# A two-block network on one core: the state heads of block one woven with the attention in a fixed period, and its turned x, B and chunk states placed later in the order

## What is computed

```python
for i in range(DEPTH):                       # DEPTH = 2
    h = rms_norm(x, norm_mix_w[i])
    proj = jnp.einsum("bld,de->ble", h, w_in[i])
    q, k, v, z, xbc_raw, dt_raw = jnp.split(proj, split_at, axis=-1)
    ...
    attn_out = blocked_gqa(q, k, v)          # 8 query heads, 2 key heads, head size 64
    ssd_out = ssd_mixer(z, xbc_raw, dt_raw, conv_w[i], conv_b[i], ...)
    x = x + jnp.einsum("ble,ed->bld", jnp.concatenate([attn_out, ssd_out], -1), w_out[i])
    h = rms_norm(x, norm_ffn_w[i])
    x = x + (silu(h @ w_gate[i]) * (h @ w_up[i])) @ w_down[i]
```

## Time and profile before

| | |
|---|---|
| median of 3 runs | 3262.46 us (3255.55 to 3265.68) |
| profiled execution | 3256.09 us, of which the traced span is 3254.3 us |
| TensorE busy | 3041.3 us (93% of the span) |
| VectorE, ScalarE, GpSimd busy | 1896.9, 1123.2, 87.5 us |
| mean granted TensorE clock | 0.968 |

### The profile page before, as it was taken

How to read it: one execution, slowest core, us unless ns; L and a number is a source line. 1 busy time by engine, 2 the same in 40 slices (tenths; PEclk the granted TensorE clock), 3 DMA queues, 4 the chain that set the end, 5 groups by cost and what they waited for, 6 DMA issues and landing times. The chain is left out here.

```text
span 3254.3 us, 39867 instructions
## 1 busy us (share of the span) xinstructions
PE 3041.3 (93%) x16294; PEld 2688.1 (83%) x16294; DVE 1896.9 (58%) x2835; ACT 1123.2 (35%) x1660; POOL 87.5 (3%) x72
## 2 busy tenths in 40 slices
PE   7988999999879999999967779999999999999998
PEld 6767888887768888899955369999999978799997
DVE  5755775856555878765546664552554365455464
ACT  4443422234444222343335123221222345433232
POOL 0031000000140000000000000000000000000000
PEclk9998999999989999999979889999999999999999
DMA  3100554521102655422100111121112210223232
GB/s 129 46 33 15 177 177 141 197 84 59 40 14 88 197 181 188 149 65 98 65 13 1 57 71 52 65 69 57 64 67 64 95 51 1 68 81 103 85 99 84
DMA packets 73137, 275.80 MB, mean 85 GB/s; under 512 B 7835, under 2 KB 11419, under 8 KB 71804
## 3 DMA queue, kind: packets, MB, share of 16 engines
q1 hardware_dynamic: 72956, 273.25, 25.3%
HBM read 264.83 MB, written 8.39 MB: 84 GB/s over the span
## 5 line engine op out<-in xcount | busy, mean ns | idle before, releaser
L122 PE MATMUL banks<-normed_hi,weights_hi 128*128 128x384 f32 (+2 forms) x2672 | 888.2, 338 | 11.5 <-DVE normed_lo L866 11.5
L123 PE MATMUL banks<-normed_lo,weights_hi 128*128 128x384 f32 (+2 forms) x2672 | 885.4, 337 | 0.0
L104 ACT ACTIVATE weights_hi<-weights_raw 128x1024 fp32r<-128x1024 f32 (+3 forms) x365 | 395.6, 1084 | 1244.9 <-PE banks L125 1218.4
L125 PE MATMUL banks<-normed_hi,weights_lo 128*128 128x384 f32 (+2 forms) x2672 | 743.5, 338 | 0.0
L110 DVE TENSOR_TENSOR weights_lo<-weights_raw,weights_hi 128x1024 fp32r<-128x1024 f32 (+3 forms) x365 | 459.7, 1259 | 139.4 <-ACT weights_hi L104 136.0
L122 PEld LDWEIGHTS banks<-normed_hi,weights_hi 128*128 128x128 f32 x2672 | 504.5, 189 | 39.7 <-DVE normed_lo L866 12.2
L123 PEld LDWEIGHTS banks<-normed_lo,weights_hi 128*128 128x128 f32 x2672 | 506.4, 190 | 27.3
L125 PEld LDWEIGHTS banks<-normed_hi,weights_lo 128*128 128x128 f32 x2672 | 473.8, 190 | 27.6
L123 PE MATMUL banks<-hidden_lo,weights_hi 128*128 128x512 f32 (+1 forms) x880 | 323.0, 367 | 0.0
L122 PE MATMUL banks<-hidden_hi,weights_hi 128*128 128x512 f32 (+1 forms) x880 | 323.0, 367 | 0.0
L125 PE MATMUL banks<-hidden_hi,weights_lo 128*128 128x512 f32 (+1 forms) x880 | 294.7, 367 | 0.0
(11 more groups left out here) (439 smaller groups left out, 4224.0 us busy)
## 6 DMA issues: line engine op xcount, KB each, us to landing
weights_raw<-in_w_up SPq DMA_DIRECT2D x176, 512.0 KB, 3.4
ada_tiles<-in_ada SPq DMA_DIRECT2D x96, 512.0 KB, 3.5
weights_raw<-in_w_down SPq DMA_DIRECT2D x64, 704.0 KB, 4.0
weights_raw<-in_w_in SPq DMA_DIRECT2D x67, 512.0 KB, 3.4
weights_raw<-in_w_out SPq DMA_DIRECT2D x32, 512.0 KB, 3.4
x_kept<-x SPq DMA_DIRECT2D x2, 3072.0 KB, 10.5
x<-x_kept SPq DMA_DIRECT2D x1, 3072.0 KB, 9.7
weights_raw<-in_mla_down SPq DMA_DIRECT2D x6, 512.0 KB, 3.4
```

The source lines that it names most:

```text
L104: act.activation(self.hi[:, n % 2, 0:w], self.raw[:, n % 2, 0:w], ACT.Copy).then_inc(self.high_ready, 1)
L122: pe.matmul(out, self.hi[:, s, m], xh, start=k == 0, stop=False)
L123: pe.matmul(out, self.hi[:, s, m], xl, start=False, stop=False)
L125: mm = pe.matmul(out, self.lo[:, s, m], xh, start=False, stop=k == kt - 1)
```

## The change

It adds, removes and alters no instruction; it alters the numbers by which `weave` orders them, in `FirstMix`, and so in both layers. First, attention steps 21 to 28 are no longer due every 1.2 units but one per head, at `head(h) + 0.5` (`slot`), with their exponential, maximum and rows moved into the next head's period (`follows`). Second, within a period of a head the order is laid down anew on TensorE (`decays` of the next head ahead of the attention step), ScalarE (`diagonal` ahead of the exponential, then `decay` of the next head) and VectorE (`diag` first, `skip` of the head before ahead of `weigh`). Third, the turned x are due every 1.2 instead of every 0.6 units, and the turned B, the B, C scores and the chunk states 0.7 later.

```diff
-        self.pace, self.lag = 1.2, 1.0
+        self.pace, self.lag, self.free = 1.2, 1.0, 21
...
+    def slot(self, n):
+
+        if n < self.free:
+            return self.pace * n + self.lag + 0.5
+        if n < self.free + 8:
+            return self.head(n - self.free) + 0.5
+        return self.head(8) + 0.5 + self.pace * (n - self.free - 8)
+
+    def follows(self, n, early, late):
+
+        return self.head(n - self.free + 1) + late if self.free <= n < self.free + 8 else self.slot(n) + early
...
-            yield self.pace * n + self.lag + 0.5
+            yield self.slot(n)
...
-            yield self.pace * n + self.lag + 0.8
+            if self.free <= n < self.free + 8:
+                yield self.slot(n) + 0.4
+                copy(n)
+            yield self.follows(n, 0.3, 0.4)
             if n + 2 < STEPS:
                 exp(n + 2)
-            yield self.pace * n + self.lag + 0.9
-            copy(n)
+            if not self.free <= n < self.free + 8:
+                yield self.slot(n) + 0.4
+                copy(n)
             if n % 2 and n >= 5:
-                yield self.pace * n + self.lag + 1.1
+                yield self.follows(n, 0.6, 0.42)
...
-            yield self.pace * n + self.lag + 0.7
+            yield self.follows(n, 0.2, 0.3)
             if n + 2 < STEPS:
                 top(n + 2)
             if n:
-                yield self.pace * n + self.lag + 0.85
+                yield self.follows(n, 0.35, 0.35)
                 rows(n - 1)
             if n % 2 and n >= 5:
-                yield self.pace * n + self.lag + 1.2
+                yield self.follows(n, 0.7, 0.55)
...
-            yield 12 + 0.6 * t
+            yield 12 + 1.2 * t
...
-            yield 19.3 + 0.5 * g
+            yield 20.0 + 0.5 * g
...
-            yield 20.3 + 0.5 * g
+            yield 21.0 + 0.5 * g
...
-            yield 21.3 + 0.5 * i
+            yield 22.0 + 0.5 * i
             states(i)
-        h0 = self.head(0)
-        yield h0
+        yield self.head(0)
         decays(0)
         for h in range(8):
             if h + 1 < 8:
-                yield self.head(h + 1)
+                yield self.head(h) + 0.3
                 decays(h + 1)
-            yield self.head(h) + 1.1
+            yield self.head(h + 1) + 0.05
             outputs(h)
...
+        yield self.head(0) + 0.05
+        decay(0)
         for h in range(8):
-            yield self.head(h) + 0.2
-            decay(h)
-            yield self.head(h) + 0.5
+            yield self.head(h) + 0.25
             diagonal(h)
+            if h + 1 < 8:
+                yield self.head(h) + 0.6
+                decay(h + 1)
...
-        return max(self.done(18) + 0.9 + 0.1 * n, self.head(2 * n + 1) + 2.0)
+        return max(self.done(18) + 0.9 + 0.1 * n, self.head(2 * n + 2) + 0.65)
...
-            yield self.head(h) + 0.35
+            yield self.head(h) + 0.1
             diag(h)
+            if h:
+                yield self.head(h) + 0.6
+                skip(h - 1)
             yield self.head(h) + 0.8
             weigh(h)
-            if h:
-                yield self.head(h) + 0.9
-                skip(h - 1)
-        yield self.head(7) + 1.4
+        yield self.head(8) + 0.6
         skip(7)
```

20 lines of the change are left out of this document (10 added, 10 removed).

## The result

The changed kernel took 3222.05 us in the median of 4 runs (3220.82 to 3222.51). The kernel before, timed beside it, took 3259.63 (3255.55 to 3265.68, 4 runs). The ratio is 0.9883, 95% interval 0.9869 to 0.9897: 37.6 us faster. The profiled execution of after took 3222.1 us around a span of 3220.3; that of before 3256.1 around 3254.3.

What follows compares the result with a forecast made beforehand. TensorE, busy for 93% of the span, was taken as the bound. Heads 15.9, end 1.7 and ahead of the heads 8.5 make 26.1 us a layer, 52 for two: 3262.5 - 52 = 3210.5, said as 3210, range 3197 to 3236.

Steps and rivals of the forecast that it cites:

- The heads: Eight head periods after the first spread sums: TensorE bounds each at 6.17 us, gaining 15.9 us a layer.
- the end: Stretch behind the heads: one attention step fewer is left there, gaining 1.7 us a layer, between 0 and 2.1.
- ahead of the heads: Stretch before the first spread sums: waits at 128, 148 and 169 us go, gaining 8.5 us a layer, between 3 and 10.
- the forecast case: Main case for the whole kernel: from 3197 to 3226 us (18 us a layer), chance 0.64.
- three waits: TensorE waits ahead of the heads: 1.56 us at 128.15, 3.02 at 148.07, 2.79 at 169.05; all were to go.
- The lock: Rival in the heads: GpSimd's exclusive lock delays each `weigh` to 2.2 to 2.6 us; 3228 to 3240 us, chance 0.15.
- margin of only 0.2 us: In the heads: in periods with a gate, `weigh` is late next after TensorE, by this margin.
- Lockstep at half clock: Rival in the heads: outputs wait for VectorE's chain, TensorE idles at 1.2 GHz, period 10.3 us; 3278 us, chance 0.04.
- Half of it: Rival: VectorE can't keep pace between 128 and 166 us, heads start each at 6.8; 16 us a layer, 3230, chance 0.15.

## Why the prediction was right, and where it was not

Forecast 3210, measured 3222, inside the range of 3197 to 3236; the gain was 37.6 us where 52 were worked out. The heads, the largest term, held in mechanism and size; the end had the wrong sign, and the term ahead of the heads was too large. The sum lay in the range with a term of the wrong sign because the heads gave 1.6 and 1.8 us more than forecast, and because the forecast case allowed for as little as 18 us a layer; that part is luck.

- **The heads, right.** 15.9 forecast, 17.5 and 17.7 measured. The last output lies 54.5 us behind the first sums, where 56 was said; the period is 5.94 and not 6.17, because the steps and sums pass a little closer than in the earlier trace rows; the median of `weigh` is 1.214 us; outputs 2 to 7 have no wait over 0.3. The clock was to be 0.95 or more and is 0.94: it is low at the start, where the second sums take 1.22 us behind a wait of 3.41, a wait that the working saw coming.
- **The end, wrong: the step that failed.** "Eight instead of seven attention steps lie in the heads, so one fewer is left behind them: 2.1 us of TensorE [...] so I take 1.7, between 0 and 2.1." The step did leave (15 records fewer), and the end became 4.3 and 4.5 us longer. The argument counted TensorE's work and not the chain on the other engines, which the change itself had reordered: TensorE asks for the turn of step 30 0.6 us sooner, the copy comes 1.2 us later behind the moved gate and squares, and a wait of 0.49 us grew to 2.32. The bound of 0 from below was unfounded: nothing excluded a loss. The sums at half clock are the larger part, 3.3 us in layer 0; with the wait merely filled, 3.0 and 2.6 us came back, and with the gate later 4.5 and 2.1. That the wait decides when the clock falls is not shown: with the copy first and the wait gone, the sums still ran half at 1.2 GHz.
- **Ahead of the heads, too large.** 8.5 forecast, 7.0 and 4.0 measured. Two of its three waits went as worked out, and the new wait before the second turned B is 1.88 us where 1.8 was said; the turned pairs and the states wait 0.69 each, said as 0.7. The third was misread: "The 3.02 us at 148.07 is a probability copy late behind four products x·dt within two units of VectorE". The copy has its input 7 us before it runs. It stands on ScalarE behind an exponential that waits for VectorE; moving two of the four products made that exponential earlier by little, and 2.36 us stayed. Putting the copy first removed the wait, in the kernel before (12.5 us) as in the changed one (21.3 with the end). The layers differ by the clock, 0.98 and 0.94 over this stretch with the same waits, and no run shows why.
- **The rivals.** The lock did not decide, and the extra mask shows how near it was. The "margin of only 0.2 us" in periods with a gate was nothing in fact: `weigh` ends at 227.48 and output 2 starts at 227.53, with its weight load 0.23 us late for `weigh`; without a gate 0.5 us is left (232.85 and 233.36). That room to spare lay on GpSimd instead: it waits 1.4 to 1.9 us in most periods for the decays, and it is its own `scaled` that is now caught behind `weigh` (1.77 in place of 1.00 us) and can bear it. Lockstep at half clock did not come. "Half of it" (VectorE can't keep its pace between 128 and 166 us) had the place right and half of the mechanism: VectorE is late with the maximum, but TensorE waited for a copy that did not need it, and the heads did not start at 6.8. Its time, 3230, is nearer to the measured one than 3210.
- **The sum.** 26.1 a layer against 20.2 and 17.2, and some 3 us lost in stages with the same instructions, which no step had foreseen.

## What to carry to other kernels

When an edit takes work off the busiest engine in a stretch, ask of each wait there what chain on the other engines it is the end of: with less work in front of it, the same chain shows as a longer wait, and an instruction that moved into the chain lengthens it. On an in-order engine, put the instruction whose input is ready ahead of the one whose input is late; "waits for X on ScalarE" in a profile is often the wait of whatever stands before X. And a wait of 2 us has no fixed price, since half clock may follow it up to the next stretch of full work: here the 3.02 us at 148 us cost about twice its length, the end 4.3 us for 1.8 of added wait, and the 3.41 us ahead of the sums of head 1 next to nothing.

## What the runs showed of the hardware

- **The clock falls while TensorE is busy.** In the end with the copy first everywhere the first 16 sums of one column take 1.90 to 2.02 us and the next 16 take 3.5, with no idle time between them and with a wait of only 0.35 us ahead. With the last gate later there is a wait of 1.12 us ahead in both layers; the 32 sums take 3.88 us in layer 0 and 6.20 in layer 1. A mean of the granted clock over a stretch is no measure of the idle time in it, then, nor does the length of a wait say what follows. The runs can't say what does.
- **The clock differs far from the edit.** A stretch with the same instructions near 1800 us took 10 us more in one traced execution (granted clock 0.65, not 0.84), and a chain of stages of some 680 us differs by 2.3 and 2.6 us between two pairs of kernels that are the same there. Whether the change or the execution brings this about is not shown. A gain of a few microseconds is read at the place of the edit, by arrival times, before the total is believed or not.
- **The lock goes both ways.** A `weigh` asked for during a mask ends 1.08 us behind the mask, in the earlier trace rows and with the extra mask. A `scaled` of GpSimd asked for 0.29 us behind the start of a `weigh` takes 1.79 in place of 1.00 us, on these timelines of after, VectorE and then GpSimd:

```profile
238.13 1.22 DVE L2260 TENSOR_TENSOR diagonal<-diagonal,bc_scores 128x1024 f32<-128x1024 f32 x1
```

```profile
238.42 1.79 POOL L2343 TENSOR_TENSOR scaled_c<-conv,decay_rows 128x384 f32<-128x384 f32 x1 [1.87 <-ACT decay_rows L2175]
```

The Trainium skill (SBUF — State Buffer, section "SBUF: two separate sides") says that whichever of the two starts first has the shared ports for its whole instruction; both cases agree, with these numbers. What decides is then which comes first, and the change turned the order round: before, `weigh` came second and TensorE waited; now `scaled` does, and outputs 2 to 7 don't wait for it.
